# Latent attention of a fused block: V is the stationary operand, divided probabilities move, two heads share the array's two column halves

## The reference, cut to what matters

```python
q = rms_norm(q, g_qn[l]); k = rms_norm(k, g_kn[l])           # then rotary on the last 32
s = jnp.einsum('bhqd,bhkd->bhqk', qblk, kt).astype(jnp.float32) * scale
p = jax.nn.softmax(s, axis=-1).astype(vt.dtype)
attn = jnp.einsum('bhqk,bhkd->bqhd', p, vt)                   # 256 tokens x (8 heads x 64)
u_attn = (attn * jax.nn.silu(z_attn)) @ w_attn_out[l]
```

## Time and profile before

| what | value |
|---|---|
| median of 3 runs | 1087.27 us (1086.77 to 1088.87) |
| span of the profiled execution | 1085.8 us |
| TensorE busy | 1078.1 us (99%) |
| VectorE busy | 794.0 us (73%) |
| ScalarE busy | 592.3 us (55%) |
| chain that ended last | TensorE 96% |

### The profile page before, as it was taken

One profiled execution on the slowest core, in us unless ns is written; L12 is line 12 of the kernel. 1 busy time (PEld: TensorE's weight loads), 2 busy tenths in 40 slices (PEclk: granted clock), 3 DMA queues, 4 the chain that ended last, 5 costly groups with the idle time before them and its releaser, 6 DMA issues.

```text
span 1085.8 us, 20858 instructions
## 1 busy us (share of the span) xinstructions
PE 1078.1 (99%) x8460; PEld 1023.1 (94%) x8460; DVE 794.0 (73%) x1117; ACT 592.3 (55%) x842; POOL 0.2 (0%) x4
## 2 busy tenths in 40 slices
PE   8999999999999999999999999999999999999999
PEld 6999999999999999999999998999999799999998
DVE  5665657989989867778778555775655887997784
ACT  5544445678643345878445556544444575655461
POOL 0000000000000000000000000000000000000000
DMA  9765555455443364444556533465556355543341
GB/s 354 277 231 194 193 187 201 157 198 189 161 150 117 117 212 158 156 159 147 204 173 237 201 100 133 146 220 205 186 183 209 118 176 206 183 156 117 118 155 40
DMA packets 29169, 190.69 MB, mean 176 GB/s; under 512 B 3656, under 2 KB 4457, under 8 KB 7274
## 3 DMA queue, kind: packets, MB, share of 16 engines
q1 hardware_dynamic: 26480, 182.53, 48.5%
q10 hardware_dynamic: 2618, 7.14, 1.9%
HBM read 188.61 MB, written 1.05 MB: 175 GB/s over the span
## 4 chain that ended last, share of the span: by engine, by line
PE 96%; DVE 1%; DMA 1%; ACT 1%; issue 1%; SPq 0%; ACTq 0%; DVEq 0%
PE bank L525 16%; PE bank L526 16%; PE bank L527 16%; PE bank L537 11%; PE bank L538 11%; PE bank L539 11%; PE bank L624 3%; PE bank L760 1%; PE bank L871 1%; DMA sb_w_raw<-in_w 1%; PE bank L1019 1%; PE bank L708 1%; PE bank L1239 1%; PE bank L1031 1%; PE bank L1075 1%; PE bank L1097 1%
## 5 line engine op out<-in xcount | busy, mean ns | idle before, releaser
L2084 DVE TENSOR_TENSOR sb_w_lo<-sb_w_raw,sb_w_hi 128x2048 fp32r<-128x2048 f32 x169 | 386.4, 2289 | 127.7 <-ACT sb_w_hi L1367 127.0
L1367 ACT ACTIVATE sb_w_hi<-sb_w_raw 128x2048 fp32r<-128x2048 f32 x169 | 322.9, 1911 | 30.7 <-PE bank L527 27.5
L525 PE MATMUL bank<-sb_hT_hi,sb_w_hi 128*128 128x256 f32 (+1 forms) x816 | 225.8, 277 | 0.0
L527 PE MATMUL bank<-sb_hT_hi,sb_w_lo 128*128 128x256 f32 (+1 forms) x816 | 225.7, 277 | 0.0
L526 PE MATMUL bank<-sb_hT_lo,sb_w_hi 128*128 128x256 f32 (+1 forms) x816 | 225.6, 276 | 0.0
L537 PE MATMUL bank<-sb_hT_hi,sb_w_hi 128*128 128x256 f32 (+2 forms) x744 | 212.7, 286 | 0.2 <-DVE sb_w_lo L2092 0.2
L538 PE MATMUL bank<-sb_hT_lo,sb_w_hi 128*128 128x256 f32 (+2 forms) x744 | 206.2, 277 | 0.0
L539 PE MATMUL bank<-sb_hT_hi,sb_w_lo 128*128 128x256 f32 x744 | 205.9, 277 | 0.0
L525 PEld LDWEIGHTS bank<-sb_hT_hi,sb_w_hi 128*128 128x128 f32 (+1 forms) x816 | 152.8, 187 | 0.0
L526 PEld LDWEIGHTS bank<-sb_hT_lo,sb_w_hi 128*128 128x128 f32 (+1 forms) x816 | 152.6, 187 | 0.0
L527 PEld LDWEIGHTS bank<-sb_hT_hi,sb_w_lo 128*128 128x128 f32 (+1 forms) x816 | 152.5, 187 | 0.1
(11 more groups left out here) (513 smaller groups left out, 2106.8 us busy)
## 6 DMA issues: line engine op xcount, KB each, us to landing
sb_w_raw<-in_w SPq DMA_DIRECT2D x169, 1024.0 KB, 5.0
sb_w_raw<-in_w SPq DMA_DIRECT2D x4, 512.0 KB, 7.6
sb_hT<-in_xT SPq DMA_DIRECT2D x2, 512.0 KB, 5.4
sb_x<-in_x SPq DMA_DIRECT2D x2, 512.0 KB, 11.5
sb_mem_xn<-in_mem ACTq DMA_DIRECT2D x1, 1024.0 KB, 5.9
sb_mem_T<-in_memT ACTq DMA_DIRECT2D x1, 1024.0 KB, 8.2
sb_post_g<-in_ffn_post_g ACTq DMA_DIRECT2D x2, 512.0 KB, 5.7
sb_decay<-in_c_decay ACTq DMA_DIRECT2D x1, 768.0 KB, 5.4
```

The costliest lines, as they stand in the source:

```text
L525: pe.matmul(o, a_hi, b_hi, start=first, stop=False)
L527: return pe.matmul(o, a_lo, b_hi, start=False, stop=last)
L1367: act.activation(w_hi[b % STAGES][:], w_raw[b % RING][:], ACT.Copy).then_inc(w_hi_in, 1)
L2084: tt(w_lo[b % STAGES][:], w_raw[b % RING][:], f32(w_hi[b % STAGES][:]), ALU.subtract).then_inc(w_lo_in, 1)
```

## The change

`mla_out(c)` now takes a pair of heads: V (128 x 64) is stationary, m_PT moves with 256 columns, and head 2c writes partitions 0 to 63, head 2c + 1 partitions 64 to 127 of bank 5. The result has channels on partitions already; `at_scale`, `at_turn` and at_tok are gone, and `at_gate` reads bank 5. m_PT has two buffers. Since columns are now tokens, the division by the row sums comes before the transposes: `rows_scale(h)` on VectorE divides m_p in place and raises `m_scaled`, for which `mla_turn(h)` waits in place of the exponentials' read of the scores. `rows_scale(h)` for h = 0 .. 6 stands at the head of VectorE's iteration h + 1; `rows_scale(7)` stands in iteration 7, behind the row maximum of head 7. `mla_out(c)` stands in TensorE's iterations 3, 5, 7 and 9.

```diff
@@ TensorE
             def mla_turn(h):
-                wait_read(pe, f"ms{h}")
+                pe.wait_ge(S("m_scaled"), h + 1)
                 o = claim(f"mPT{h}", 4)
...
-            def mla_out(h):
-                wait_read(pe, f"mPT{h}")
-                if h % 2 == 0:
-                    claim(f"mo{h // 2}", 5)
-                for q in range(2):
-                    at = q * P + h % 2 * V_DIM
-                    for kb in range(2):
-                        mm = pe.matmul(banks[5][:, at:at + V_DIM], m_PT[:, kb, q * P:(q + 1) * P], mv[:, kb, h, :],
+            def mla_out(c):
+                for h in range(2):
+                    wait_read(pe, f"mPT{2 * c + h}")
+                o = claim(f"mo{c}", 5)
+                for kb in range(2):
+                    for h in range(2):
+                        mm = pe.matmul(o[h * V_DIM:(h + 1) * V_DIM, 0:SEQ], mv[:, kb, 2 * c + h, :], m_PT[h][:, kb, :],
                                        start=kb == 0, stop=kb == 1)
-                if h % 2:
-                    ends(mm, f"mo{h // 2}")
-            def at_turn(c, bank):
-                wait_read(pe, f"mo{c}")
-                o = claim(f"aT{c}", bank)
-                for t in range(TOK):
-                    mm = turn(o[:, t * P:(t + 1) * P], at_tok[:, t].rearrange("p h d -> p (h d)"))
-                ends(mm, f"aT{c}")
+                ends(mm, f"mo{c}")
...
-                if i in (4, 6):
-                    at_turn(i // 2 - 2, (FIRST["steps"] + i + 2) % 3)
-                elif i == 8:
-                    at_turn(2, 2)
-                if i >= 2:
-                    mla_out(i - 2)
+                if i in (3, 5, 7, 9):
+                    mla_out(i // 2 - 1)
@@ ScalarE
+                    if i >= 3:
+                        full(act, f"mo{(i - 3) // 2}")
-                    copy(f"mPT{i - 1}", m_PT[:], two(o))
+                    copy(f"mPT{i - 1}", m_PT[(i - 1) % 2][:], two(o))
@@ VectorE
-            def at_scale(c):
-                wait_read(dve, f"ms{2 * c + 1}")
-                heads = slice(2 * c, 2 * c + 2)
-                link(dve.reciprocal(m_rec[:, :, heads], m_sum[:, :, heads]))
+            def rows_scale(h):
+                wait_read(dve, f"ms{h}")
+                link(dve.reciprocal(m_rec[:, :, h:h + 1], m_sum[:, :, h:h + 1]))
+                for q in range(2):
+                    ins = ts(m_p[:, h % 2, q, :], m_p[:, h % 2, q, :], m_rec[:, q, h:h + 1], None, ALU.mult)
+                ins.then_inc(S("m_scaled"), 1)
...
             for i in range(MLA_HEADS + 2):
                 c = (i - 3) // 2
+                if 1 <= i < MLA_HEADS:
+                    rows_scale(i - 1)
...
                 if i == 7:
+                    rows_scale(7)
                     at_gate(2)
```

More of the change, by code:

```diff
@@ L453, in program @@
         m_rs = place(61.6875, "m_rs", [P, TOK * MLA_HEADS])
-        at_tok = place(48, "at_tok", [P, TOK, 2, V_DIM])
         msq = place(72, "msq", [P, TOK, MLA_HEADS, QK_DIM])
@@ L458, in program @@
         dft_a = place(78, "dft_a", [P, 4, P])
-        m_PT = place(82, "m_PT", [P, 2, SEQ])
+        m_PT = [place(82, "m_PT0", [P, 2, SEQ]), place(80, "m_PT1", [P, 2, SEQ])]
         hy_re = place(32, "hy_re", [P, 2, HY])
@@ L1317, in _ @@
                              None if i == 9 else hy_ready,
-                             between=(lambda: at_turn(3, 7)) if i == 9 else lambda: mla_turn(7))
+                             between=None if i == 9 else lambda: mla_turn(7))
                 if 1 <= i < MLA_HEADS:
@@ L2047, in _ @@
                     c = (i - 3) // 2
-                    wait_read(act, f"aT{c}")
+                    wait_read(act, f"mo{c}")
                     act.activation(at_hi[:, c, :], z_at[:, c, :], ACT.Copy).then_inc(S("at_hi"), 1)
@@ L2884, in softmax_rows, with at_gate @@
                 stt(m_st[:, 1, :], m_st[:, 0, :], -1.0, scale, ALU.mult, ALU.mult).then_inc(S("m_max"), 1)
-            def at_scale(c):
-                wait_read(dve, f"ms{2 * c + 1}")
-                heads = slice(2 * c, 2 * c + 2)
-                link(dve.reciprocal(m_rec[:, :, heads], m_sum[:, :, heads]))
-                o = full(dve, f"mo{c}")
-                read(tt(at_tok[:], o[:, 0:SEQ].rearrange("p (t h d) -> p t h d", t=TOK, h=2),
-                        m_rec[:, :, heads].unsqueeze(3).to_broadcast([P, TOK, 2, V_DIM]), ALU.mult), f"mo{c}")
-            def at_gate(c):
-                o = full(dve, f"aT{c}")
-                read(tt(z_at[:, c, :], o[:, 0:SEQ], z_at[:, c, :], ALU.mult), f"aT{c}")
+            def rows_scale(h):
[4 more added lines that the diff above has]
+                ins.then_inc(S("m_scaled"), 1)
+            def at_gate(c):
+                o = full(dve, f"mo{c}")
+                read(tt(z_at[:, c, :], o[:, 0:SEQ], z_at[:, c, :], ALU.mult), f"mo{c}")
             def at_low(c):
@@ L2947, in _ @@
                 elif i == 7:
-                    at_scale(2)
                     hyena_gate(1)
@@ L2955, in _ @@
                     at_gate(c)
-                if i in (3, 5):
-                    at_scale(c)
                 if i < MLA_HEADS:
@@ L2977, in _ @@
                 if i == 8:
-                    at_scale(3)
                     dve.wait_ge(S("gate2"), 1)
```

## The result

The changed kernel takes 1100.7 us (median of 4 runs, 1100.31 to 1101.42), the kernel before beside it 1088.07 us (4 runs, 1086.77 to 1089.36). The ratio is 1.012, with a 95% interval of 1.0109 to 1.0132. The forecast was 1097.9, with a range of 1095 to 1101.5. In the profiled execution the span went from 1085.8 to 1098.5 us, 12.7 more.

A forecast was written before the change was run, and what follows sets the result against it. TensorE, busy 1078.1 of 1085.8 us, was taken as the bound. Waits of 13.5 less 4.0 of own work, plus 1.1 for the clock, gave 1096.4; the median's 1.5 above the span made 1097.9 us, range 1095 to 1101.5.

The forecast's parts named there:

- wait, head 0: TensorE before head 0's transposes: stands until VectorE, free only behind a weight block, has divided; 5.4 us.
- wait, head 1: TensorE before head 1's transposes: VectorE's chain from row maximum to scaling takes 7.0 us against 5.3; wait 1.75 us.
- TensorE's own work: Old V products and transposes of attended rows go, 7.6 us; four paired products of 0.9 us come: -4.0 us.
- Rival (a): The division's wait costs nothing because VectorE gets there in time; only TensorE's saving stays: 1083.3 us, 4%.
- rival (f): Later waits partly vanish, only the first two left (7.2 us): 1091.6 us, 5%.
- Head 7 ... about 0.4 us: Transposes inside the first hyena output block wait for head 7's own exponentials and scaling: about 0.4 us.
- I take nothing for the column edges.: V product on TensorE: entering and leaving column halves costs nothing, with 0.4 us kept as the upper bound.
- rival (b): V product's column halves do not overlap, 1.7 us per pair instead of 0.9: 1100.4 us, 12%.
- Rival (c): Entering and leaving the half array drains it, 1.3 us per pair: 1099.1 us, 8%.
- I take +1.1: TensorE's clock falls in head 0's wait, so the transposes and scores behind it take 1.1 us more.
- Rival (d): TensorE's clock stays at its full level through the waits: 1096.8 us, 15%.
- Rival (e): The clock falls behind head 5's wait as well, 2.4 us more: 1100.3 us, 11%.

The follow-up runs named there:

- the kernel without division: Changed kernel with the division by the row sums left out, transposes waiting only for the exponentials: 1085.63 us, ratio 0.9972 to 0.9991.
- the run with one half: Both heads' V products in one column half: without division, in the other matmul order, 1089.05 us (overlap); in the changed kernel 1104.76 us (clock).
- the two runs on the halves: Kernel without division: V product's four matmuls ordered head by head, 1086.54 us; in that order with both heads in one column half, 1089.05 us.

## Why the prediction was right, and where its sizes were off

The time lies in the range, and the mechanism is the one that was forecast: the division's place in VectorE's order sets the waits, the halves overlap, and the clock falls with the first wait. Two of its terms were mis-sized by 1 us or more, head 7 and the edges of the V product. The terms, in us, from start to start in the changed kernel's trace:

| term | predicted | measured |
|---|---|---|
| wait, head 0 | 5.4 | 5.37 |
| wait, head 1 | 1.75 | 1.19 |
| waits, heads 2 and 6 | 0 | 0 |
| wait, head 3 | 0.3 | 0 |
| wait, head 4 | 2.3 | 1.90 |
| wait, head 5 | 3.4 | 3.39 |
| first hyena output block and head 7 | 0.4 | 0.84 + 0.98 |
| low clock | 1.1 | 1.9 |
| TensorE's own work | -4.0 | -3.0 |
| sum, to compare with the span's +12.7 | +10.6 | +12.6 |
| median above the span | 1.5 | 2.2 |

By the usual distances of the kernel without division (0.31 us in front of head 4's turn, 0.17 in front of head 7's) heads 4 and 7 waited 1.80 and 0.92, and the sum is 12.4.

**The waits** were read rightly from VectorE's order: 0.02 us off at head 0, and 0.01 at head 5. Rival (a) is out, and rival (f) too: no later wait vanished but the 0.3 at head 3.

**"Head 7 ... about 0.4 us"** is the step that failed most, by 1.4 us. I let the wait for the block's inputs cover it, and priced those at nothing. They cost 0.84 (1.05 from start to start, 0.21 usual there), and as much in the kernel without division (1.06), so that part comes of TensorE's smaller work and not of the division. And head 7's own chain is serial: its row maximum stands on VectorE behind the four low parts of the hyena output (L2940, 1.43 us), and then exponentials, reciprocal and scalings follow, with one half of the block to hide them.

**"I take nothing for the column edges."** The records of a V product: first distance 0.21 us from the matmul before instead of 0.12, 0.26 for the first step instead of 0.21, 0.31 for the last, and 0.17 to the second transpose instead of 0.11. A pair costs 1.15 us by these records, not 0.9. That halves overlap, rival (b)'s question, is shown by the run with one half. Rival (c) is half true: the edges cost some 0.25 us per pair, below the 0.4 of the row halves. The Trainium skill (TensorEngine Tiling (Array Packing), Key Properties) says that a change of tiling mode drains the TensorE, and with those 0.25 us this trace agrees. It also says there that tiles work independently, and the two runs on the halves agree.

**"I take +1.1"** for the clock. It fell, as taken, and the transposes and scores behind the wait lost 1.14 us (0.909 and 1.353 us instead of 0.44 and 0.68). The block lost 0.78 where I had 1.3. I had let the low level begin at the end of the wait and last at most 4.9 us; it lasted 6.8, but nearly half of that, 3.3 us, lay inside the wait. My claim that the wait of head 1 covers this came true, in the form that head 1's wait is 1.19 and not 1.75. Both together were 2.85 predicted and 3.09 measured: VectorE's chain to head 1 takes 7.03 us from its maximum (984.86 to 991.89), where I had 7.0, and it started 1.36 us late for the clock, not 1.1. So in the table these two lines are one error of 0.2 us, not two. Rival (d) is out. Rival (e) did not come in the changed kernel, but came in the run with one half, at the same place, for 1.4 us where 2.4 had been forecast.

The forecast ended 2.8 us low: 1.4 from head 7 and the block in front of it, 1.0 from the edges, 0.2 from the clock with head 1, less 0.7 at heads 3 and 4, which makes 1.9 of the span's 2.1, and 0.7 because the median lay 2.2 above the span. That last part is no error about the change: every run's time lies 1.8 above its own span, and the profiled execution was the fastest of the four (1100.31). Against the kernel before beside it, 1088.07, the change cost 12.6 us where 10.6 was forecast.

## What to carry to other kernels

Where one engine is full, a new dependency can cost it the distance in the other engine's program order, even if that engine's busy share is far from full (73% here): find the instruction behind which the new one is queued, and count from there. Price a saving on the full engine by where it lies: right in front of a wait it buys nothing (here 2.4 to 3 of 3 us came back as waiting). If a wait can't be avoided, move its consumer one iteration on and its producer in front of the longest instruction near it, and then look again at every other product of the producer's queue, since each of them is now late by the work put in.

## What the runs showed of the hardware

- **The clock can fall for a shorter idle stretch than the one I took.** It fell within idle stretches of 5.21 and 3.23 us, and in the run with one half only after an idle stretch of 3.04 us had ended, with TensorE at work for 0.84 us again (the rows below). It did not fall within or behind another stretch of 3.23 (head 5 of the changed kernel, granted 1.00 on both sides). Around the 5.21 us the rows at 0.71 and 0.78 make 6.8 us at the lower level (5.60 times 0.58 and 8.00 times 0.44); around the 3.23 us, 0.75 over 6.80 us makes 3.4; behind the 3.04 us it was 3.4 as well.

```profile
1032.02:1035.06 3.04, 0.00 (x1) 0.00 (x1) 3.00 (x5) 0.84 (x2) 0.00 (x0) 1.00 0.00 0
1035.06:1035.90 0.84, 0.84 (x6) 0.81 (x7) 0.84 (x2) 0.15 (x1) 0.00 (x0) 1.00 0.95 127
1035.90:1039.30 3.40, 3.40 (x16) 3.12 (x15) 2.61 (x6) 1.17 (x4) 0.00 (x0) 0.50 0.69 277
```

- **Column halves with f32 operands run side by side** in both orders of issue that were run, at 0.21 us per record of 256 columns in each.
- **GpSimd beside VectorE.** Two scalings of 128x256 took 1.82 us alone and up to 5.87 beside VectorE's products of two operands. VectorE's lost some 0.2 us each at most: 2.44 instead of 2.29 for a low half, 1.30 instead of 1.22, and 0.88 instead of 0.68 for the product below, a third more. The Trainium skill (SBUF — State Buffer, SBUF: two separate sides) says that such a VectorE operation and a GpSimd one exclude each other from a shared port for a whole instruction. The trace agrees on GpSimd's side (one scaling begun beside a low half took 2.88 us instead of 0.92), and GpSimd lost far the more.

```profile
1024.77 0.88 DVE L2857 TENSOR_TENSOR sb_hy_im<-sb_spec 128x512 f32<-128x512 f32 x1
```
